# One weight stream through eleven fixed buffers in a two-layer kernel with experts

## The reference

```
for layer in range(2):
    x = x + mixer[layer](rmsnorm(x))        # even: gated recurrence + sparse attention; odd: windowed attention
    x = x + hier_moe(rmsnorm(x))            # 32 experts, each token goes to 2

def expert_block(xblk, e):
    hid = silu(xblk @ w_gate[e]) * (xblk @ w_up[e])     # 1024 -> 512
    return hid @ w_down[e]                              # 512 -> 1024
```

## Time and profile before

| | |
|---|---|
| median of 3 runs | 1223.64 us (1223.16 to 1228.26) |
| the profiled execution | 1222.98 us, of which the span is 1221.2 |
| busy in the span | PE 893.0, PEld 638.1, DVE 338.0, ACT 186.3, POOL 28.5 us |
| moved by DMA | 440.77 MB, mean 361 GB/s |
| mean granted clock of TensorE | 0.902 |

### The profile page before, as it was taken

The page is one execution under the profiler, slowest core; times in us unless marked ns, Lnnn a source line. Parts: engine busy times, 40 slices in busy tenths (PEclk is TensorE's granted clock), DMA queues, the critical chain, the costliest instruction groups (busy, mean ns, idle before and its releaser), DMA issues.

```text
span 1221.2 us, 27980 instructions
## 1 busy us (share of the span) xinstructions
PE 893.0 (73%) x12510; PEld 638.1 (52%) x12510; DVE 338.0 (28%) x867; ACT 186.3 (15%) x470; POOL 28.5 (2%) x34
## 2 busy tenths in 40 slices
PE   6999997786576767675758989776757576666655
PEld 6766765664454455453535565665545354444443
DVE  2476554222121212121204562421212021211211
ACT  3333422110000000000003442111000010000000
POOL 2121000000000000000000000000000000000000
PEclk9999998998988888888989999798988798988888
DMA  9845135989999999999999723789999999999996
GB/s 394 354 174 205 69 139 201 390 324 428 428 428 429 429 429 428 428 429 428 428 429 427 316 109 142 309 350 414 429 428 429 429 429 428 427 428 428 429 429 264
DMA packets 31146, 440.77 MB, mean 361 GB/s; under 512 B 3584, under 2 KB 3712, under 8 KB 4480
## 3 DMA queue, kind: packets, MB, share of 16 engines
q1 hardware_dynamic: 29088, 417.35, 81.5%
q10 hardware_dynamic: 2016, 22.80, 4.7%
HBM read 439.09 MB, written 1.05 MB: 360 GB/s over the span
## 4 chain that ended last, share of the span: by engine, by line
DMA 56%; PE 35%; DVE 5%; ACT 2%; issue 2%; SPq 0%; DVEq 0%; ACTq 0%
DMA ring<-weights 55%; PE PS L396 11%; PE PS L736 6%; PE PS L747 6%; PE PS L404 2%; PE PS L715 2%; DVE side L1161 1%; PE PS L757 1%; PE PS L431 1%; PE PS L466 1%; ACT side L970 1%; DVE st L1375 1%; PE PS L689 1%; DVE scr L1161 1%; PE PS L385 1%
## 5 line engine op out<-in xcount | busy, mean ns | idle before, releaser
L736 PE MATMUL PS<-ring,probT 128*32 128x128 f32 x7680 | 280.6, 310 | 167.9 <-DMA ring<-weights 164.4
L736 PEld LDWEIGHTS PS<-ring,probT 128*32 128x32 f32 x7680 | 245.3, 125 | 209.8 <-DMA ring<-weights 198.3
L747 PE MATMUL PS<-ring,scr 128*32 128x256 f32 x1984 | 147.3, 447 | 53.6 <-DMA ring<-weights 40.8
L396 PE MATMUL PS<-ring,side 128*128 128x512 f32 (+1 forms) x352 | 148.2, 574 | 2.3 <-ACT side L876 1.4
L1161 DVE TENSOR_TENSOR scr<-scr,PS 128x128 f32<-128x128 f32 x64 | 18.4, 288 | 420.1 <-ACT scr L1085 420.1
L747 PEld LDWEIGHTS PS<-ring,scr 128*32 128x32 f32 x1984 | 72.3, 124 | 105.5 <-DMA ring<-weights 50.5
L1594 DVE COPY probT<-PS 32x256 f32<-32x256 f32 x128 | 54.3, 425 | 189.5 <-PE PS L747 188.6
L396 PEld LDWEIGHTS PS<-ring,side 128*128 128x128 f32 x352 | 65.3, 190 | 70.1 <-issue 69.3
L1085 ACT ACTIVATE scr<-PS 128x128 f32<-128x128 f32 x64 | 17.7, 277 | 455.1 <-PE PS L736 455.1
L1089 ACT ACTIVATE probT<-PS 32x256 f32<-32x256 f32 x128 | 47.7, 373 | 256.5 <-PE PS L747 255.7
L757 PE MATMUL PS<-probT,scr 128*128 128x512 f32 x128 | 64.0, 635 | 15.7 <-DVE probT L1594 15.7
(11 more groups left out here) (215 smaller groups left out, 620.1 us busy)
## 6 DMA issues: line engine op xcount, KB each, us to landing
ring<-weights SPq DMA_DIRECT2D x198, 2048.0 KB, 25.7
side<-weights ACTq DMA_DIRECT2D x10, 2048.0 KB, 8.1
x<-x_in SPq DMA_DIRECT2D x2, 512.0 KB, 4.1
out<-x SPq DMA_DIRECT2D x2, 512.0 KB, 2.6
TB<-table ACTq DMA_DIRECT2D x1, 973.5 KB, 11.2
SM<-small ACTq DMA_DIRECT2D x1, 732.0 KB, 17.5
TB<-table ACTq DMA_DIRECT2D x1, 64.0 KB, 3.8
SM<-small ACTq DMA_DIRECT2D x1, 20.0 KB, 4.8
```

The lines of the kernel that those rows point to most:

```text
L396: mm = pe.matmul(PS[:, bank, 0:n], hT[:, k, t * P:(t + 1) * P], w[:, k, 0:n], start=(k == 0), stop=(k == KD - 1))
L736: mm = pe.matmul(PS[f * CAP:(f + 1) * CAP, b, up * P:(up + 1) * P], gatherT[:, k, tok], w[:, k, f * P:(f + 1) * P], start=(k == 0), stop=( ...
L747: mm = pe.matmul(PS[q * CAP:(q + 1) * CAP, 4 + e % 2, 0:256], hidT[:, e % 2, f * CAP:(f + 1) * CAP], w[:, f, q * 256:(q + 1) * 256], start ...
```

## The change

All eleven buffers are numbered as one set: slots 0 to 6 are the ring (now seven, side4 has become a ring slot), 7 to 10 are side0 to side3. All weights are loaded from SyncE's queue; ScalarE's `fill_side` goes. The even mixer uses the seven ring slots in turn. In the expert layers each j has a fixed buffer (`MOE_SLOT`), the same for every quad, and its next load waits for the same j of the quad before. As 12 chunks have 11 buffers, j = 5 and j = 11 share slot 7 (`TWICE`). In the loop the order of issue is: j = 0 to 3 of quad i, then j = 11 of quad i - 1, then j = 4, 5, ..., 10 of quad i. The first 11 chunks of a layer are issued in the order of j, each after a wait of its own (`free0`, `free1`). `chunk_done` now counts all chunks. POOL's restoring waits for the first transposes after the first experts.

```
-NSLOT = 6
+NRING, NSIDE = 7, 4
+NSLOT = NRING + NSIDE
-SIDE = (6, 7, 8, 9, 10)
+DONE_MOE = (EV_CHUNKS, EV_CHUNKS + OD_CHUNKS)
+TWICE = 7
+MOE_SLOT = ((4, 5, 6, 0, 1, TWICE, 8, 2, 3, 9, 10, TWICE), (2, 3, 4, 5, 6, TWICE, 8, 0, 1, 9, 10, TWICE))
+ODD_SLOT = (4, 5, 6, 0, 1)
+EARLY = 4
...
+            def load(slot, source):
+                return sp.dma_start(buffer(slot), source).then_inc(w_landed[slot], 16)
...
+                def again(j, i):
+                    sp.wait_ge(chunk_done, done - QC + QC * i + (QC if j == 5 else j + 1))
+                    load(slots[j], row(j, i))
+
+                def last_of(i):
+                    sp.wait_ge(chunk_done, done + 6 - QC + QC * i)
+                    load(TWICE, row(QC - 1, i + QUADS - 1))
...
+                with sp.Fori(at + 1, end) as i:
+                    for j in range(EARLY):
+                        again(j, i)
+                    last_of(i)
+                    for j in range(EARLY, QC - 1):
+                        again(j, i)
+                last_of(end)
...
             for c in range(EV_CHUNKS):
-                chunk(c, weights[c])
-            end0 = quads(MOE0, None, RING_MOE0, 0)
+                if c >= NRING:
+                    sp.wait_ge(chunk_done, c - NRING + 1)
+                load(even_slot(c), weights[c])
+            free0 = [(chunk_done, 5), (chunk_done, 6), (chunk_done, 7), (chunk_done, 8), (chunk_done, 9),
+                     (cat_ready, 1), (scored, U1), (chunk_done, 10), (chunk_done, 11), (routed, 1), (m_pick, 1)]
...
+            free1 = [(chunk_done, odd - 4), (chunk_done, odd - 3), (chunk_done, odd + 1), (chunk_done, odd + 2),
+                     (chunk_done, odd + 3), (chunk_done, odd), (scored, len(units)), (chunk_done, odd + 4),
+                     (chunk_done, odd + 5), (routed, 2), (m_pick, end0 + 2)]
...
-            pool.wait_ge(side_done, len(SIDE))
+            pool.wait_ge(hT_turned, 2 * TT * 2 + 1)
...
-            def fill_side(layer, n, free, count):
-                act.wait_ge(free, count)
-                act.dma_start(side[n][:, :], weights[(MOE0, MOE1)[layer] + SIDE[n]]).then_inc(side_landed[n], 16)
```

More of the change, by code:

```diff
@@ L51, with even_slot, loads_before @@
 THR = CAP
-def ring_number(base, j, first):
-    return base + j - (0 if first and j < SIDE[0] else len(SIDE))
+def even_slot(c):
+    return c % NRING
+def loads_before(slot, layer):
+    even = len([c for c in range(EV_CHUNKS) if even_slot(c) == slot])
+    return even + (1 if layer == 1 and slot in ODD_SLOT else 0)
 def columns(parts):
@@ L88, in sem @@
             return ctx.enter_context(nc.semaphore(name))
-        ring = sb("ring", [P, NSLOT, CW])
+        ring = sb("ring", [P, NRING, CW])
         SM = sb("SM", [P, SMALL_N])
@@ L96, in build @@
         probT = sb("probT", [P, 2, 1024])
-        side = [sb(f"side{n}", [P, CW]) for n in range(len(SIDE))]
+        side = [sb(f"side{n}", [P, CW]) for n in range(NSIDE)]
         hq = side[0][:, 0:1024].rearrange("p (h t) -> p h t", h=HG_H)
@@ L171, in build, with buffer @@
         pickT = scr[:, 5 * S:6 * S]
+        def buffer(n):
+            return ring[:, n, :] if n < NRING else side[n - NRING][:, :]
         def sm(name, parts=P):
@@ L194, in build @@
         w_landed = [sem(f"w_landed{i}") for i in range(NSLOT)]
-        side_landed, side_done = [sem(f"side_landed{n}") for n in range(len(SIDE))], sem("side_done")
         chunk_done = sem("chunk_done")
@@ L273, in _, with quads, row @@
                 sp.dma_start(x[:, t, :], x_in[t * P:(t + 1) * P, :]).then_inc(x_loaded[t], 16)
[L275 to L287, removed]
+            def load(slot, source):
+                return sp.dma_start(buffer(slot), source).then_inc(w_landed[slot], 16)
+            def quads(base, first, layer):
+                done, slots = DONE_MOE[layer], MOE_SLOT[layer]
+                at = 0 if first is None else first
+                def row(j, i):
+                    return weights[bass.ds(base + j + QC * (i % QUADS), 1)].rearrange("a p n -> p (a n)")
+                def again(j, i):
[4 more added lines that the diff above has]
+                    load(TWICE, row(QC - 1, i + QUADS - 1))
                 sp.wait_ge(route_ready, layer + 1)
@@ new lines, in _ @@
+            for j, (free, count) in enumerate(free0):
+                sp.wait_ge(free, count)
+                if free is routed:
+                    sp.wait_ge(ssq_ready, 2 * TT)
+                load(MOE_SLOT[0][j], weights[MOE0 + j])
+            end0 = quads(MOE0, None, 0)
+            for k in range(OD_CHUNKS):
+                sp.wait_ge(chunk_done, DONE_ODD - QC + QC * end0 + k + 1)
+                load(ODD_SLOT[k], weights[ODD0 + k])
+            odd = DONE_ODD + QC * end0
+            free1 = [(chunk_done, odd - 4), (chunk_done, odd - 3), (chunk_done, odd + 1), (chunk_done, odd + 2),
+                     (chunk_done, odd + 3), (chunk_done, odd), (scored, len(units)), (chunk_done, odd + 4),
+                     (chunk_done, odd + 5), (routed, 2), (m_pick, end0 + 2)]
@@ L303, in _ @@
+            for j, (free, count) in enumerate(free1):
+                sp.wait_ge(free, count)
+                if free is routed:
+                    sp.wait_ge(ssq_ready, 4 * TT)
+                load(MOE_SLOT[1][j], weights[MOE1 + j])
+            end1 = quads(MOE1, end0, 1)
             for t in range(TT):
@@ L365, in _, with landed, odd_landed, moe_landed @@
         def _(pe):
[L366 to L370, removed]
+            def landed(c):
+                pe.wait_ge(w_landed[even_slot(c)], 16 * (c // NRING + 1))
+                return buffer(even_slot(c))
+            def odd_landed(k, iters):
+                slot = ODD_SLOT[k]
+                pe.wait_ge(w_landed[slot], 16 * (loads_before(slot, 0) + 1) + 16 * iters)
+                return buffer(slot)
+            def moe_landed(layer, i, j):
+                slot = MOE_SLOT[layer][j]
+                if slot == TWICE:
+                    pe.wait_ge(w_landed[slot], 32 * i + (16 if j == 5 else 32))
+                else:
+                    pe.wait_ge(w_landed[slot], 16 * (loads_before(slot, layer) + 1) + 16 * i)
+                return buffer(slot)
             def turn_tokens(u, t, half, iters=None):
@@ L503, in out_projection @@
             def out_projection(layer, t, half, c, iters, ks=range(KD)):
-                w = cols(landed(c + half, iters))
+                w = cols(landed(c + half) if layer == 0 else odd_landed(c + half, iters))
                 if half == 0:
@@ L698, in router, with quad @@
                 pe.matmul(PS[:, 7, 64:96], tb("ones"), m[:, 1, :], start=False, stop=True).then_inc(ranked, 1)
[L700 to L708, removed]
+            def quad(layer, i):
                 pe.wait_ge(m_onehot, i + 1 + layer)
@@ L729, in quad @@
                     for up in range(2):
-                        w, done = chunk_of(3 * e + up)
-                        w = cols(w)
+                        w = cols(moe_landed(layer, i, 3 * e + up))
                         for k in range(KD):
@@ L738, in quad @@
                                                start=(k == 0), stop=(k == KD - 1))
-                        mm.then_inc(done, 1)
+                        mm.then_inc(chunk_done, 1)
                     pe.wait_ge(m_hid, QE * i + e + 1)
                     pe.transpose(PS[:, b, 2 * P:3 * P], hid[:, e % 2, :], ident).then_inc(m_hid_turned, 1)
-                    w, done = chunk_of(3 * e + 2)
-                    w = w.rearrange("p (f n) -> p f n", f=4)
+                    w = moe_landed(layer, i, 3 * e + 2).rearrange("p (f n) -> p f n", f=4)
                     pe.wait_ge(m_hidT, QE * i + e + 1)
@@ L758, in quad, with experts @@
                               yq[:, half * 512:(half + 1) * 512], start=True, stop=True).then_inc(m_comb, 1)
-            def experts(layer, first, pre):
-                quad(layer, first, True, pre)
+            def experts(layer, first):
+                quad(layer, first)
                 pe.wait_ge(route_ready, layer + 1)
@@ L766, in experts @@
                 with pe.Fori(first + 1, end) as i:
-                    quad(layer, i, False, pre)
+                    quad(layer, i)
                 return end
             router(0, 9, None)
-            end0 = experts(0, 0, RING_MOE0)
+            end0 = experts(0, 0)
             for t in range(TT):
@@ L822, in _ @@
             values(U1 + 5)
-            out_projection(1, 0, 1, c0 + 3, end0, range(KD // 2))
+            out_projection(1, 0, 1, 3, end0, range(KD // 2))
             turn_cat(1, 1)
-            out_projection(1, 0, 1, c0 + 3, end0, range(KD // 2, KD))
-            router(1, c0 + 3, end0)
-            experts(1, end0, RING_MOE1)
+            out_projection(1, 0, 1, 3, end0, range(KD // 2, KD))
+            router(1, 3, end0)
+            experts(1, end0)
         @block.scalar
@@ L906, in _ @@
```

(32 more changed lines are left out.)

18 lines of the change are left out of this document (6 added, 12 removed).

## The result

1235.0 us median (1234.08 to 1237.23, 6 runs) against 1224.9 before (6 runs); ratio 1.009, 95% interval 1.0067 to 1.0112. The change is slower, as forecast, but by 10 us where 26 were forecast. The profiled execution took 1235.05 us (span 1233.3), 12.07 more than that of before.

What follows compares the result with a forecast made beforehand. DMA engines streaming weights at 428 GB/s were taken to bound the expert layers. From 1222.98 us, -5.5 and -5.6 (second dips), +0.7 (layer 1's first dip) and +37.9 (late issues) gave 1250.5, 1251 beside the median; range 1229 to 1259.

Steps and rivals of the forecast that it cites:

- the second dip: Early DMA rate drop in each expert layer, chunk 6 waiting for chunk 0; removal forecast to save 5.5 and 5.6 us.
- the sum: Forecast total: 1222.98 - 5.5 - 5.6 + 0.7 + 37.9 = 1250.5 us, or 1251 beside the median.
- next 5: Next quad's chunk 5; its load waits for this chunk 11 and holds up 6 to 10: 3.16 us a steady quad.
- T + 3.70: Forecast issue of the next quad's chunk 5, T being chunk 11's landing: 0.05 wait, 3.45 low-clock product, 0.2 to issue.
- The price of the late issue: Steady expert quads: (issue - T) + 9.25 - 9.79, T being chunk 11's landing; 3.16 us a quad, 12 times, +37.9 us.
- a price of the restart: Extra time for a load meeting an emptied queue and the stream behind it; 9.25 us taken from issue to landing.
- The lone landing, 7.6: Lowest issue-to-landing time read for a single load meeting an emptied queue, 7.6 to 9.0 us; 9.25 was taken instead.
- the rival of half the price: Steady quads lose about half: full clock 1.6 us, or lone landing at low clock 1.5 to 2.9; 1229 to 1243, chance 0.18.
- The terms at nothing: Moved POOL memsets, ten fewer ScalarE DMA issues and even-mixer load order, all forecast to cost or gain nothing.
- It holds: Claim that the late-issue price fits the earlier trace: 1.9 against 2.04 us in layer 0, 0.95 against 0.83 in layer 1.
- the two first dips: First DMA rate drops early in expert layers 0 and 1 before the change, 2.04 and 0.83 us; used to check the price.
- The page's rule: Transfer takes 2.0 us plus bytes by 436 GB/s: 6.8 us a chunk, 0.7 lost a quad, change near -2 us.

Runs made afterwards that it cites:

- two covers: Changed kernel with EARLY 3 instead of 4, so two loads stand between chunk 11 and chunk 5 of the next quad; 1213.33 us median, ratio to before 0.9921.
- held-back issues: Changed kernel with EARLY 3, next quad's chunk 5 also waiting for the first, second or third combination matmul; 1222.71, 1234.73 and 1253.76 us.
- no cover: Changed kernel with EARLY 5 instead of 4, so chunk 11 is loaded directly before chunk 5 of the next quad; 1305.68 us.
- the warm run: Changed kernel with 24 extra, unread TensorE matmuls ahead of the down product of chunk 11 in the loop; 1276.25 us.

## Why the prediction was right in part and wrong in size

- **Eleven buffers give nothing in the mixers, and remove the second dip.** Right. The version with two covers has this gain without the loss: 9.4 us under before (1213.33 against 1222.69, measured together), where the sum has 10.4 (5.5 + 5.6 - 0.7).
- **The load of next 5 holds up the queue behind it.** Right, and shown twice: an order with one more load ahead of it removes the loss, and so does another queue for this one load. With the late issue as it was, both run at 428. The held-back issues bring the loss back in the better order.
- **Six quads a layer, product at the low clock, issue at T + 3.70.** Right; measured 3.64 us and T + 3.9.
- **The price of the late issue.** This is the term that was mis-sized: "I take 9.25. A late issue then costs (issue - T) + 9.25 - 9.79", 3.16 us a quad, 37.9 in all. Measured 1.85 a quad, 22.2 in all: the issue came at T + 3.9 where the sum had T + 3.70, and the landing took 7.7 us where it had 9.25. The 15.7 us between 37.9 and 22.2 are the error. With them off, the sum gives 1234.8 (1250.5 - 15.7), and that the profiled execution took 1235.05 is in part luck, see below. The 9.25 came from loads of the kernel before that followed a standstill. Its first two, issue and time to landing:

```profile
L281 SPq DMA_DIRECT2D ring<-weights x1: 333/333/333, 262.0 to 262.0; - x1
...
DMA to landing us min/median/max: 7.9/7.9/7.9
...
L281 SPq DMA_DIRECT2D ring<-weights x1: 333/333/333, 263.8 to 263.8; - x1
...
DMA to landing us min/median/max: 12.0/12.0/12.0
```

The first landed at 269.9 like any other after a standstill, the second at 275.8, 5.9 later instead of 4.9, and the third (issued 267.2) 5.4 after that. I booked these 1.5 us as a price of the restart. In the steady quads of the changed kernel five loads follow the late one within 3.5 us, and the pace is 4.9 from the first. Why the two lost time before is not shown: they had 6.1 and 8.5 us of lead, and the two-cover kernel lost nothing at 5.9. The lone landing, 7.6, that stood beside it in the earlier trace rows was the right number; it was in the rival of half the price, at 1.5 to 2.9 us a quad, which is the case that came true.

- **The terms at nothing.** By the marks above, expert layer 0 grew by 5.90 us, for the 5.6 of the corrected terms (11.1 - 5.5). Expert layer 1 grew by 4.09, for 6.2 (11.1 + 0.7 - 5.6), and outside of them 2.07 were added that the sum had at nothing, 1.76 of them the difference between executions. The two deviations nearly cancel, which is the luck. Of the 2.1 us that layer 1 lacks, 1.4 are the last down product, which took 3.31 us before and 1.93 after; the rest was not followed:

```profile
1209.21 3.31 PE L747 MATMUL PS<-ring,scr 128*32 128x256 f32 x32 [1.85 <-DMA ring<-weights]
...
1222.63 1.93 PE L794 MATMUL PS<-side,scr 128*32 128x256 f32 x32 [1.22 <-DMA side<-weights]
```

- **"It holds", said of the two first dips.** It didn't test what I took it to test: T in that sum was itself worked out with 9.25. By its landings the fifth load of layer 0 came at 248.2 and the sixth at 253.2; next 5, issued at 251.3 with a lead of 1.9, landed at 259.7, 1.6 us late. So the issue was 3.1 us behind T and not 2.5, and the load took 8.4 us and not 9.25. The two errors nearly make each other good, since the one constant stands in the price and in T. In layer 1 T was right, and there next 5 (issue 812.7, landing 820.8) took 8.1 us and landed in pace, where the price said 0.95 us late.
- **The page's rule.** The Trainium skill, DMA: Bandwidth & Descriptors, section on the anatomy of one DMA, has 2.0 us plus bytes by 436 GB/s for the GpSimd path. The estimate of 6.8 us that it gives for a chunk is 0.9 under the 7.7 measured on SyncE's queue, and would have erred the other way: 0.7 us a quad with the sum's T + 3.70, where 1.85 were measured.

Left open: why loads with 1.9 and with 2.7 to 3.2 us of lead lose more than the time to landing explains, and why the same lead of 2.7 us lost 0.3 in one quad and 2.8 in another. Single loads behind a first dip also landed late for no reason that I can name: in the changed kernel two with 22.5 and 26.6 us of lead, by 0.9 and 0.6 us (at 291.9 and 297.5). The records of the 16 DMA engines aren't told apart in the trace.

## What to carry to other kernels

More buffers don't help a stream that already runs at its rate; they help where it stood still for want of one. When loads share one in-order queue, put the load with the latest release last or on a queue of its own, since everything behind it inherits its wait. Two uses of one buffer close together in the order need more than one transfer between them: here one transfer (4.9 us) between them was too little and two (9.8) were enough. And a constant that was fitted to a pattern isn't confirmed by a sum that uses it twice; landings can be read directly.

## What the runs showed of the hardware that was not expected

A 2 MB load took 7.6 to 7.8 us from issue to landing where the queue had run empty (the run with no cover, steady quads of layer 0), but it kept the 4.9 us of the stream only if it was issued early enough. With 5.9 us of lead, and in layer 0 with 3.8 to 4.1, nothing was lost. With 2.7 to 3.2 us, which should have been enough or all but enough by the 7.7, 0.3 to 2.8 us were lost. With 1.0 us it was 1.6 to 2.2, with 0.1 to 0.2 us 2.6 to 2.8. So the earlier issue of the warm run (lead 2.7) cost the same on average as the late one of the changed kernel (lead 1.0), 1.9 us a quad.
